# The first norm's statistics move from TensorE to ScalarE and a DRAM row

## What is computed

```python
h = rmsnorm(x, norm_mix[0])          # x * rsqrt(mean(x*x) + eps) * g
u = h @ w_in
gate_b, gate_c, v = jnp.split(u, 3, axis=-1)
z = gate_c * v
zc = conv_w[0] * zp[:, :-2] + conv_w[1] * zp[:, 1:-1] + conv_w[2] * zp[:, 2:]
x = x + (gate_b * zc) @ w_out
```

## Time and profile before

| | us |
|---|---|
| median of 3 runs | 1042.48 |
| lowest, highest | 1041.26, 1043.23 |
| span of the profiled execution, first to last instruction | 1041.8 |
| PE busy | 1032.3 (99%) |
| DVE busy | 846.8 (81%) |
| ACT busy | 598.4 (57%) |
| POOL busy | 103.6 (10%) |

### The profile page before, as it was taken

How to read it: one execution, slowest core, us unless ns; L and a number is a source line. 1 busy time by engine, 2 the same in 40 slices (tenths; PEclk the granted TensorE clock), 3 DMA queues, 4 the chain that set the end, 5 groups by cost and what they waited for, 6 DMA issues and landing times.

```text
span 1041.8 us, 15414 instructions
## 1 busy us (share of the span) xinstructions
PE 1032.3 (99%) x6104; PEld 905.4 (87%) x6104; DVE 846.8 (81%) x1185; ACT 598.4 (57%) x836; POOL 103.6 (10%) x158
## 2 busy tenths in 40 slices
PE   9999999999999999999999999999999999999997
PEld 8888888988998998998878888889888988988985
DVE  5876688699899689688987767797799798698697
ACT  6222347665584574575765655547664674674675
POOL 3453001000000000000113000000000000000003
PEclk9999999999999999999999999999999999999999
DMA  7998568326745645633998733157056547447423
GB/s 247 375 375 300 141 165 254 108 42 207 204 132 176 177 128 177 181 97 102 372 249 249 215 90 114 55 191 274 1 122 205 163 133 202 150 134 202 147 51 111
DMA packets 36998, 182.71 MB, mean 175 GB/s; under 512 B 5760, under 2 KB 5888, under 8 KB 22848
## 3 DMA queue, kind: packets, MB, share of 16 engines
q1 hardware_dynamic: 23184, 108.57, 28.8%
q0 software_dynamic: 13456, 72.64, 28.3%
q10 hardware_dynamic: 288, 0.52, 0.2%
HBM read 136.93 MB, written 27.32 MB: 158 GB/s over the span
## 4 chain that ended last, share of the span: by engine, by line
PE 93%; DVE 4%; DMA 1%; ACT 1%; issue 1%; POOL 0%; DVEq 0%; POOLq 0%; ACTq 0%
PE bank L770 29%; PE bank L771 29%; PE bank L772 29%; DMA raw<-sevens 1%; PE bank L975 1%; PE bank L953 1%; DVE w_l L1514 1%; PE bank L938 1%; PE bank L793 1%; DVE xs L1661 1%; PE bank L997 0%; DVE big L1970 0%; ACT big L1156 0%; DVE a_l L1727 0%; ACT w_h L1128 0%
## 5 line engine op out<-in xcount | busy, mean ns | idle before, releaser
L1128 ACT ACTIVATE w_h<-big 128x1024 fp32r<-128x1024 f32 x210 | 221.7, 1058 | 216.0 <-PE bank L772 215.0
L770 PE MATMUL bank<-a_h,w_h 128*128 128x256 f32 (+1 forms) x892 | 295.0, 331 | 0.0
L772 PE MATMUL bank<-a_h,w_l 128*128 128x256 f32 (+1 forms) x892 | 292.9, 328 | 0.0
L771 PE MATMUL bank<-a_l,w_h 128*128 128x256 f32 (+1 forms) x892 | 292.8, 328 | 0.0
L1514 DVE TENSOR_TENSOR w_l<-big,w_h 128x1024 fp32r<-128x1024 f32 x210 | 252.0, 1225 | 21.8 <-ACT w_h L1128 21.8
L770 PE MATMUL bank<-w_h,hx 128*128 128x512 f32 x568 | 222.1, 391 | 0.8 <-ACT big L1376 0.4
L771 PE MATMUL bank<-w_l,hx 128*128 128x512 f32 x568 | 221.2, 389 | 0.0
L772 PE MATMUL bank<-w_h,hx 128*128 128x512 f32 x568 | 221.0, 389 | 0.0
L770 PEld LDWEIGHTS bank<-a_h,w_h 128*128 128x128 f32 x892 | 169.6, 190 | 15.8 <-issue 0.2
L772 PEld LDWEIGHTS bank<-a_h,w_l 128*128 128x128 f32 x892 | 169.6, 190 | 15.0
L771 PEld LDWEIGHTS bank<-a_l,w_h 128*128 128x128 f32 x892 | 169.6, 190 | 14.7 <-issue 0.2
(11 more groups left out here) (193 smaller groups left out, 1253.6 us busy)
## 6 DMA issues: line engine op xcount, KB each, us to landing
big<-blocks SPq DMA_DIRECT2D x56, 1024.0 KB, 5.0
big<-big POOLq DMA_DIRECT2D x30, 1024.0 KB, 7.0
raw<-weights SPq DMA_DIRECT2D x52, 512.0 KB, 6.6
raw<-t_sums SPq DMA_DIRECT2D x16, 512.0 KB, 3.7
t_sums<-sevens POOLq DMA_DIRECT2D x6, 1024.0 KB, 12.6
t_sums<-t_sums POOLq DMA_DIRECT2D x6, 1024.0 KB, 12.2
raw<-sevens SPq DMA_DIRECT2D x12, 512.0 KB, 7.8
bias_tiles<-big POOLq DMA_DIRECT2D x8, 632.0 KB, 9.3
```

Source lines behind the costliest of these rows:

```text
L770: nc.tensor.matmul(dst, sh, mh, start=start, stop=False, skip_group_check=again)
L771: nc.tensor.matmul(dst, sh, ml, start=False, stop=False, skip_group_check=again)
L772: return nc.tensor.matmul(dst, sl, mh, start=False, stop=stop, skip_group_check=again)
L1128: nc.scalar.activation(wh_all[:, w % SLOTS, :], src, ACT.Copy).then_inc(w_hi, 1)
```

## The change

ACT no longer squares the slices of `xT`. SP loads `x_tok` right behind the last slice of the wave. ACT waits for all four of its loads and squares them, tokens on partitions, with the sum over the row as a by-product (`accum_out`); its half of unit 4's weights stands between the second and third square. DVE's adds of squares, PE's sums and spread, and the diagonals are gone. The four small steps on DVE end with `rstd_tok`; POOL then writes the 512 numbers to a row in DRAM, waits for it, and reads it back to all 128 partitions as `rstd`; its other transfers follow behind that. `lo(5)` moves ahead of DVE's wait for `rstd`. Units 0 to 23 use bank w % 8, so that unit w waits for `taken` w - 7, and for no other release. The `lo(w)` between the steps of the convolution stand in a new order. Eight products of `ones` and `ident` instead of eleven.

```diff
@@ -243,7 +243,7 @@
         ident = sb("ident", [P, P])
-        tok = sb("tok", [P, 5, 4])
+        tok = sb("tok", [P, 6, 4])
         sqa = sb("sqa", [P, 4, 2, 4])
@@ -297,10 +297,8 @@
         rstd = big[:, 16912:17424]
-        ssq = big[:, 17424:17936]
-        diag = ev2[1]
+        junk = [big[:, 6144 + D * t:6144 + D * (t + 1)] for t in range(4)]
         masked = big[:, 4096:4096 + 2 * BIAS_W]
-        sqx = xs.rearrange("p t (a n) -> p (t a) n", a=2)
@@ -408,6 +405,8 @@
         rows_dram = nc.dram_tensor("bias_rows", [HEADS, ROWS, 31, ROWS], f32, kind="Internal").ap()
+        rstd_dram = nc.dram_tensor("rstd_row", [4, P], f32, kind="Internal").ap()
+        rstd_row = rstd_dram.rearrange("t p -> (t p)").partition_broadcast(P)
         bias_dram = nc.dram_tensor("bias_tiles", [P, HEADS, BIAS_W], f32, kind="Internal").ap()
@@ -447,13 +446,11 @@
         sq_done = sem("sq_done")
-        ssq_added = sem("ssq_added")
-        ssq_done = sem("ssq_done")
         var_ready = sem("var_ready")
         std_ready = sem("std_ready")
-        diag_ready = sem("diag_ready")
-        spread_done = sem("spread_done")
-        rstd_ready = sem("rstd_ready")
+        rstd_tok = sem("rstd_tok")
+        rstd_out = sem("rstd_out")
+        rstd_in = sem("rstd_in")
         a_hi = sem("a_hi")
@@ -573,6 +570,8 @@
                     sp.dma_start(raw_all[:, 4 * P * k:4 * P * (k + 1)], wave[k]).then_inc(first_in[k], 16)
+            for t in range(4):
+                sp.dma_start(xs[:, t, :], x_tok[t]).then_inc(xs_in, 16)
@@ -591,10 +590,6 @@
                     sp.dma_start(raw_all[:, D * (r % 4):D * (r % 4 + 1)], ring_source(r)).then_inc(raw_in[r % 4], 16)
-                    if r == 16:
-                        sp.wait_ge(ssq_added, KT - 1)
-                        for t in range(4):
-                            sp.dma_start(xs[:, t, :], x_tok[t]).then_inc(xs_in, 16)
@@ -663,7 +658,11 @@
             pool.memset(masked, MASKED).then_inc(masks, 1)
-            pool.wait_ge(ssq_added, KT - 1)
+            pool.wait_ge(rstd_tok, 1)
+            pool.dma_start(rstd_dram.rearrange("t p -> p t"), tok[:, 3, :], allow_slow_non_contiguous=True).then_inc(rstd_out, 16)
+            pool.wait_ge(rstd_out, 16)
+            pool.dma_start(rstd, rstd_row).then_inc(rstd_in, 16)
+            pool.wait_ge(rstd_in, 16)
             for r in range(ROWS):
@@ -993,7 +992,7 @@
             pe.wait_ge(const_ready, 3)
-            for _ in range(11):
+            for _ in range(8):
                 nc.tensor.matmul(bank[5][:, 0:P], ones[:], ident[:], start=True, stop=True)
@@ -1019,21 +1018,10 @@
                     last.then_inc(wave_done, 1)
-                if k == KT - 2:
-                    pe.wait_ge(ssq_added, KT - 1)
-                    for t in range(4):
-                        last = nc.tensor.matmul(sums[:, t:t + 1], ssq[:, P * t:P * t + P], ones[:, 0:1],
-                                                start=True, stop=True)
-                    last.then_inc(ssq_done, 1)
-            pe.wait_ge(diag_ready, 1)
-            nc.tensor.matmul(spread[:], ones[:], diag, start=True, stop=True).then_inc(spread_done, 1)
-            unit(4, 4)
-            for w in range(5, W_OUT):
-                if w < 20:
-                    pe.wait_ge(taken, w - 3)
-                else:
-                    pe.wait_ge(h_ready, w - 19)
-                unit(w, w % 4)
+            for w in range(4, W_OUT):
+                if w >= 8:
+                    pe.wait_ge(taken, w - 7)
+                unit(w, w % 8)
             second(0)
@@ -1340,11 +1328,14 @@
                     nc.scalar.activation(wave_h[:, :, k, :], stage(k), ACT.Copy).then_inc(piece_hi if k < 4 else w_hi, 1)
-                nc.scalar.activation(sqx[:, k, :], xT[:, k, :], ACT.Square).then_inc(sq_done, 1)
-
-            act.wait_ge(raw_in[0], 16)
-            act.wait_ge(wave_done, 1)
-            nc.scalar.activation(wh_all[:, 0, 0:512], raw_all[:, 0:512], ACT.Copy).then_inc(half_hi, 1)
+
+            act.wait_ge(xs_in, 16 * 4)
+            for t in range(4):
+                if t == 2:
+                    act.wait_ge(raw_in[0], 16)
+                    act.wait_ge(wave_done, 1)
+                    nc.scalar.activation(wh_all[:, 0, 0:512], raw_all[:, 0:512], ACT.Copy).then_inc(half_hi, 1)
+                nc.scalar.activation(junk[t], xs[:, t, :], ACT.Square, accum_out=tok[:, 5, t:t + 1]).then_inc(sq_done, 1)
             act.wait_ge(var_ready, 1)
@@ -1826,12 +1817,6 @@
-            def add_square(k):
-                dve.wait_ge(sq_done, k + 1)
-                if k >= 4:
-                    dve.wait_ge(ssq_added, k - 3)
-                nc.vector.tensor_tensor(sqx[:, k % 2, :], sqx[:, k % 2, :], sqx[:, k, :], ALU.add).then_inc(ssq_added, 1)
-
             dve.wait_ge(piece_hi, 1)
@@ -1847,45 +1832,36 @@
                                             ).then_inc(piece_split if k < 4 else w_split, 1)
-                if k >= 3:
-                    add_square(k - 1)
-            add_square(KT - 1)
-            dve.wait_ge(ssq_added, KT - 2)
-            nc.vector.tensor_tensor(ssq, sqx[:, 0, :], sqx[:, 1, :], ALU.add).then_inc(ssq_added, 1)
             dve.wait_ge(half_hi, 1)
...
-            dve.wait_ge(ssq_done, 1)
-            nc.vector.tensor_scalar(tok[:, 0, :], sums, 1.0 / D, EPS, ALU.mult, ALU.add).then_inc(var_ready, 1)
+            dve.wait_ge(sq_done, 4)
+            nc.vector.tensor_scalar(tok[:, 0, :], tok[:, 5, :], 1.0 / D, EPS, ALU.mult, ALU.add).then_inc(var_ready, 1)
             dve.wait_ge(std_ready, 1)
...
                                                 in1=tok[:, 0, :], op0=ALU.mult, op1=ALU.mult))
-            link(nc.vector.scalar_tensor_tensor(out=tok[:, 3, :], in0=tok[:, 3, :], scalar=1.5,
-                                                in1=tok[:, 2, :], op0=ALU.add, op1=ALU.mult))
-            for t in range(4):
-                last = nc.vector.tensor_scalar(diag[:, P * t:P * t + P], ident[:], tok[:, 3, t:t + 1], None, ALU.mult)
-            last.then_inc(diag_ready, 1)
+            nc.vector.scalar_tensor_tensor(out=tok[:, 3, :], in0=tok[:, 3, :], scalar=1.5,
+                                           in1=tok[:, 2, :], op0=ALU.add, op1=ALU.mult).then_inc(rstd_tok, 1)
             dve.wait_ge(w_hi, 5)
...
                                     ALU.subtract).then_inc(w_split, 1)
-            dve.wait_ge(spread_done, 1)
-            nc.vector.tensor_copy(rstd, spread[:]).then_inc(rstd_ready, 1)
-            dve.wait_ge(rstd_ready, 1)
+            lo(5)
+            dve.wait_ge(rstd_in, 16)
             dve.wait_ge(pad_zero, 1)
...
                 w = W_CV + 2 * m
-                scaled(w, 4 if w == 4 else w % 4, ev[0])
-                if m == 1:
+                scaled(w, w % 8, ev[0])
+                if m == 0:
                     lo(6)
-                elif m > 1:
+                elif m > 2:
                     lo(w + 3)
-                scaled(w + 1, (w + 1) % 4, ev[1])
-                if m == 0:
-                    lo(5)
-                elif m > 1:
+                scaled(w + 1, (w + 1) % 8, ev[1])
+                if m < 2:
+                    lo(w + 7 - m)
+                elif m > 2:
                     lo(w + 4)
@@ -1901,7 +1877,7 @@
                 dve.wait_ge(unit_done, w + 1)
-                nc.vector.tensor_tensor(hraw[:, m, :], bank[w % 4][:], hraw[:, m, :], ALU.mult).then_inc(h_ready, 1)
+                nc.vector.tensor_tensor(hraw[:, m, :], bank[w % 8][:], hraw[:, m, :], ALU.mult).then_inc(h_ready, 1)
                 lo(w + 3)
...
                     sums_of_y(0, m - 1)
```

More of the change, by code:

```diff
@@ L376, in encoder @@
         attn_last = bank[7]
-        sums, spread = bank[7][:, 0:4], bank[6]
         def norm_banks(n, half):
```

## The result

The changed kernel takes 1047.77 us (median of 5 runs, 1046.94 to 1048.27) beside 1043.23 for the kernel before on the same chip: ratio 1.0048, 95% interval 1.0037 to 1.0059. It is 0.5% slower; 2.4 us less had been forecast. The profiled execution has a span of 1046.3 us, 4.5 more than before.

The account below looks back on a forecast made before the run. PE, busy 99% of the span, was taken to bound the kernel. Gains of 0.90 + 0.87 + 0.65 = 2.4 us, all else hidden, took 1042.48 to 1040.1 us, range 1038.9 to 1041.8.

Parts of the forecast that it names:

- Sums and spread: Taking the sums and the spread off PE, around unit 4, gains 0.90 and 0.87 us, together 1.77 us.
- Warm-up: Three fewer warm-up products at PE's start gain 0.65 us, between 0 and 1.28, part lost to the low clock.
- Rival D: At PE's start the clock rises later by as much as PE starts earlier: gain 1.77, 1040.7 us; chance 0.05.
- x_tok and ACT: Before unit 4: xs in at 19.5 us (20.3 at worst), ACT's squares in time, nothing lost, margin 0.6 us for x_tok.
- The DRAM row: POOL's store and read-back take 2.5 + 3.5 us, giving rstd at 32.7 us, between 31.6 and 35.3; no gain.
- rival C: DRAM round trip over 10.5 us, rstd later than 37.1, lo(9) held, price 1:1 beyond: 1044.4 us; chance 0.05.
- What eight banks cover: PE runs units 4 to 7 without release; lo(9) for unit 9 is tightest, so rstd may come until 34.7 us.
- POOL's queue: POOL's bias transfers, out blocks and gains start 12 us late, at 32.8 instead of 20.64, and cost nothing.

Follow-up runs that it names:

- e2_fill: The changed kernel with 18 products of ones and ident added on PE between units 5 and 6; 1049.92 us, ratio 1.0075.
- the probes above: Small stores to spare DRAM rows added on POOL's queue in the attention, in two kernels with lo(6) and lo(7) before the rstd wait; spans 1040.8 and 1040.6 us.
- e9_store_only: The changed kernel with the row stored as 128 pieces of 16 bytes and one strided copy by DVE into rstd; 1044.0 us, ratio 1.0010.
- e8_probe: e1_lo_ahead with eight stores to spare DRAM rows, in four layouts, added on POOL's queue in the attention; one execution, span 1040.8 us.
- e1_lo_ahead: The changed kernel with lo(6) and lo(7) ahead of DVE's wait for rstd and lo(8) to lo(12) earlier; 1042.21 us, ratio 0.9987.

## Why the prediction was wrong

**Sums and spread, 1.77 us: right.** The second product of unit 4 was 2.08 us earlier, of which 0.39 came from the warm-up (k = 1 started at 9.13 instead of 9.52) and 0.08 was lost in front of it: 1.77.

**Warm-up, 0.65 us: right in kind, 0.4 in this profile.** The first real product started at 5.50 and not at 5.24, because x's first slice came later (ACT's copy at 4.64 instead of 4.38). With eight products the other profiles gained 0.3 to 1.2 us. The rise did not wait for a count of products: in e2_fill the four of line 1001 took 1.17 us right behind eight warm-up products, in the changed kernel 1.95. Rival D did not occur.

**x_tok and ACT: nearly right.** xs was in at 20.3, the worst value named, and cost PE 0.08 us before unit 4. rstd_tok came at 27.5 instead of 26.6.

**The DRAM row: the step that failed.** "Nearest is L668, eight transfers of 15.5 KB in short pieces on the same queue", 2.5 us. The store took 9.1, outside the bounds of 2.2 to 3.0, and just under the far bound of 9.3 that I had named and given to rival C alone. L668 resembled it only in count. By its slices (line 668) each transfer is 496 pieces of 32 bytes from DRAM to DRAM, which lie dense too, but with two pieces to 64 bytes instead of sixteen; the probes above show that for pieces of 4 bytes this decides (9.1 us dense, 3.4 and 2.6 at a step of 32). The fixed 2.5 us of my sum had no term for it. The read-back (4.1 for 3.5) was sized well. rstd: 41.3 instead of 32.7, of which 6.6 is the store, 0.9 the later rstd_tok, 0.6 the read-back and 0.5 the hand-overs. The Trainium skill's rules ("DMA: Bandwidth & Descriptors": a descriptor for each element in "Rules for kernel authors", some 2 us of fixed cost in "Anatomy of one DMA — SWDGE (gpsimd) path") gave an estimate of 4.6 us for both hops. The two took 13.2 us together, so this case does not agree with it; of the stores, only the spaced ones (2.1 to 2.6 us) come near the 2 us.

**What eight banks cover: right.** The limit of 34.7 us for rstd and the price of 1:1 beyond it hold: lo(9) ended 20.5 us behind rstd (20.4 forecast), and 41.3 - 34.7 = 6.6 us were lost, the 4.05 + 2.4 + 0.1 above. The first gap stood before unit 6 instead of unit 9, because rstd passed lo(6)'s own limit of 37.0 too (38.8 less 1.8). A fall of the clock was not in my account. In this kernel it took the place of the second gap and added nothing, as e2_fill shows; in e9_store_only it cost 1.6 us by itself.

**POOL's queue: right in that it cost nothing.** Its bulk started 21 us late instead of 12, again by the late row, and L697 still waited 20.05 us for ACT (33.12 before).

**The rival.** C was the true case, with its condition (a round trip of over 10.5 us; it was 13.2) and its rate: 1042.5 - 2.4 + 6.6 = 1046.7 against 1047.8 measured (4.2 above the median before, against 4.5). Its stated cause was wrong: "only a crowded DMA does that", but in e8_probe the same store took 8.4 us with 61 GB/s moving in all, and the read-back, which C made slow, took 4.1 and not 9.3. I gave it 0.05 and the range left it out. No row showed a store like this one, and its narrow range came from a single row of another layout. The margin was only 2.0 us while the far bound lay some 7 us off, so C deserved a far larger chance, and the range should have reached it.

## What to carry to other kernels

Before numbers go through DRAM to be spread over partitions, time that very store: its layout can decide more than its size, and 2 KB can cost 9 us. Queue nothing behind such a wait that another engine needs and that does not itself need the result; two subtractions moved ahead of it, with the next four moved forward, were worth 5.6 us by the mark. When a gap and a fall of the clock stand together, look for the next wait behind them before adding up what their removal would bring.

## What the runs showed of the hardware that was not expected

- 512 stores of 4 bytes, dense in DRAM, land in 8.4 to 11.2 us; the same 256 bytes apart in 2.3 to 2.6; 128 of 16 bytes dense in 4.4 to 5.1.
- Other transfers beside a small store go with 1 to 2 us more: 128 pieces of 16 bytes at a step of 256 bytes took 2.2 us alone and 4.2 beside 130 GB/s.
- With PE idle from 39.3 to 43.2 us, the granted clock fell to its lower level before PE began again, and a gap of 2.2 us (e9_store_only) was followed by such a stretch too. It stayed up after a gap of 2.3 us before unit 9 (e2_fill), one of 0.9 us (e1_lo_ahead), and one of 5.7 us of which unread products filled 4.2 (e2_fill, before unit 6).
- A multiplication of 128x512 on DVE took 1.06 us instead of 0.69 with one operand read at a step of 16 bytes; a plain copy with that step took 0.62.
